# Gated feed-forward, last group: the order of the short pair and the full pairs

## The reference, cut to what matters

```python
x = layer_norm(ALPHA * x + merged @ w_out[l], ln1_g[l], ln1_b[l])
u = causal_dwconv(x @ w_up[l], f_conv_w[l], f_conv_b[l])
u_gate, u_val = jnp.split(u, 2, -1)
x = layer_norm(ALPHA * x + (jax.nn.silu(u_gate) * u_val) @ w_down[l], ln2_g[l], ln2_b[l])
```

## Time and profile before

| | |
|---|---|
| median of 3 runs | 2588.08 us |
| lowest, highest | 2584.64, 2588.22 us |
| span of the profiled execution | 2591.1 us |
| own time of the profiled execution | none given beside its span |
| PE, POOL, DVE, ACT busy | 97%, 60%, 53%, 26% of the span |
| mean granted clock of TensorE | 0.987 |

### The profile page before, as it was taken

How to read it: one execution, slowest core, us unless ns; L and a number is a source line. 1 busy time by engine, 2 the same in 40 slices (tenths; PEclk the granted TensorE clock), 3 DMA queues, 4 the chain that set the end, 5 groups by cost and what they waited for, 6 DMA issues and landing times.

```text
span 2591.1 us, 30721 instructions
## 1 busy us (share of the span) xinstructions
PE 2517.8 (97%) x11112; PEld 1992.6 (77%) x11112; DVE 1369.7 (53%) x1916; ACT 667.4 (26%) x1101; POOL 1563.9 (60%) x1061
## 2 busy tenths in 40 slices
PE   7999999999999999999999999999999999999998
PEld 6875688888877776688867886767888787888885
DVE  5975683221379999968214335444356134534344
ACT  3006621100254434421022114223114212200002
POOL 2640256766779898667633765624763567566663
PEclk8999999999999999999999999999999999999998
DMA  9620132233222322122320231312331223233221
GB/s 299 222 92 1 57 123 83 96 97 98 98 82 82 97 81 65 53 98 98 112 67 33 98 98 51 98 49 66 98 91 56 65 81 98 81 97 98 96 76 44
DMA packets 224141, 231.46 MB, mean 89 GB/s; under 512 B 12219, under 2 KB 213788, under 8 KB 223900
## 3 DMA queue, kind: packets, MB, share of 16 engines
q1 hardware_dynamic: 221104, 229.33, 28.0%
q10 hardware_dynamic: 2924, 0.66, 0.1%
HBM read 227.87 MB, written 2.10 MB: 89 GB/s over the span
## 4 chain that ended last, share of the span: by engine, by line
PE 85%; DVE 8%; DVEq 2%; ACT 2%; POOLq 1%; issue 1%; DMA 1%; POOL 0%; ACTq 0%; SPq 0%
PE PS L1540 64%; PE PS L1487 7%; PE PS L1348 3%; DVE PS L3076 3%; PE PS L2136 1%; DVEq L3078 1%; PE PS L1007 1%; PE PS L2338 1%; PE PS L2355 1%; PE PS L2127 1%; DVE PS L3120 1%; PE PS L2723 1%; DMA spare<-in_ada_w 1%; PE PS L1777 0%; POOLq L3065 0%
## 5 line engine op out<-in xcount | busy, mean ns | idle before, releaser
L1461 POOL TENSOR_TENSOR Wl<-raw,Wh 128x512 fp32r<-128x512 f32 (+2 forms) x764 | 1035.2, 1386 | 28.3 <-issue 4.1
L1455 POOL TENSOR_SCALAR Wh<-raw 128x2048 fp32r<-128x2048 f32 (+1 forms) x195 | 367.7, 1886 | 816.3 <-issue 378.4
L1540 PE MATMUL PS<-Hh,Wh 128*128 128x512 f32 x1936 | 765.5, 395 | 30.2 <-POOL Wl L1461 21.0
L1540 PE MATMUL PS<-Hl,Wh 128*128 128x512 f32 x1936 | 758.8, 392 | 0.0
L1540 PE MATMUL PS<-Hh,Wl 128*128 128x512 f32 x1936 | 758.1, 392 | 0.0
L1540 PEld LDWEIGHTS PS<-Hh,Wh 128*128 128x128 f32 x1936 | 366.2, 189 | 117.5 <-POOL Wl L1461 20.3
L1540 PEld LDWEIGHTS PS<-Hh,Wl 128*128 128x128 f32 x1936 | 366.2, 189 | 77.8
L1540 PEld LDWEIGHTS PS<-Hl,Wh 128*128 128x128 f32 x1936 | 366.5, 189 | 77.3 <-issue 1.7
L1540 PE MATMUL PS<-Bh,Wh 128*128 128x512 f32 x688 | 271.4, 394 | 2.7 <-DVE Bl L3372 2.1
L1540 PE MATMUL PS<-Bh,Wl 128*128 128x512 f32 x688 | 269.7, 392 | 0.0
L1540 PE MATMUL PS<-Bl,Wh 128*128 128x512 f32 x688 | 269.6, 392 | 0.0
(11 more groups left out here) (505 smaller groups left out, 3015.2 us busy)
## 6 DMA issues: line engine op xcount, KB each, us to landing
raw<-in_w_in SPq DMA_DIRECT2D x44, 1024.0 KB, 5.5
raw<-in_w_ff SPq DMA_DIRECT2D x32, 1024.0 KB, 5.3
raw<-in_conv_w_in SPq DMA_DIRECT2D x24, 1024.0 KB, 5.2
raw<-in_ret_w_in SPq DMA_DIRECT2D x24, 1024.0 KB, 5.1
spare<-in_ada_w SPq DMA_DIRECT2D x20, 1024.0 KB, 9.0
raw<-in_w_up SPq DMA_DIRECT2D x20, 1024.0 KB, 5.3
raw<-in_w_out SPq DMA_DIRECT2D x8, 1024.0 KB, 4.9
raw<-in_conv_w_out SPq DMA_DIRECT2D x8, 1024.0 KB, 5.0
```

Source lines behind the costliest of these rows:

```text
L1455: pool.tensor_scalar(st.Wh[0:rows, slot, k, 0:cols], st.raw_slot(slot)[0:rows, k, 0:cols], 1.0, 1.0, ALU.mult, ALU.mult)
L1461: ins = pool.tensor_tensor(st.Wl[0:rows, slot, k, 0:cols], st.raw_slot(slot)[0:rows, k, 0:cols], st.Wh[0:rows, slot, k, 0:cols].bitcast(F3 ...
L1540: mm = pe.matmul(out, lhs, rhs, start=(k == parts[0][0] and n == 0), stop=(k == parts[-1][0] and n == 2))
```

## The change

In a group with a rest the short pair is put ahead of the full pairs, and the down-projection of that group takes the chunks in the order 4, 0, 1, 2, 3, with the 64-row chunk 5 behind them as before. In groups without a rest nothing changes. The functions called (`pair`, `tiles`, `kparts`) are unchanged.

```diff
         ready = first_ready if g == 0 else None
-        segs = [pair(g, 0, full, TW, ready)]
-        if rem:
-            segs.append(pair(g, 2 * full, 1, rem, None, join=P < rem <= P + P // 2))
-
-        def made(k, segs=segs, full=full):
-            return segs[0].result_ready(k) if k < 2 * full else segs[1].result_ready(k - 2 * full)
-        steps += segs
-        steps.append(tiles(wd, B, 4, 0, row0=g * D, rows=rows, ready=made,
-                           dve=add_to_x(st, x_scale=ALPHA if g == 0 else 1.0)))
+        short = [pair(g, 2 * full, 1, rem, ready, join=P < rem <= P + P // 2)] if rem else []
+        long = pair(g, 0, full, TW, None if short else ready)
+
+        def made(k, long=long, short=short, full=full):
+            return long.result_ready(k) if k < 2 * full else short[0].result_ready(k - 2 * full)
+        steps += [*short, long]
+        down = tiles(wd, B, 4, 0, row0=g * D, rows=rows, ready=made,
+                     dve=add_to_x(st, x_scale=ALPHA if g == 0 else 1.0))
+        if short:
+            down.k_order = [2 * full, *range(2 * full)]
+        steps.append(down)
```

## The result

The changed kernel runs in 2591.81 us (median of 21 runs, 2588.72 to 2595.53), the kernel before, beside it, in 2588.38 (21 runs, 2584.58 to 2591.40). The ratio is 1.0014, 95% interval 1.0009 to 1.0020: slower by 3.4 us, a loss that 21 runs of each resolve and that is under the 0.2% named in the prediction. Forecast was 2591.8.

The account below looks back on a forecast made before the run. PE, busy 97% of the span, was taken as the bound. New costs of 10.0 us against 7.9 gave +2.1; 1.6 for runs lacking the old slow clock made +3.7: 2591.8 us, range 2587.3 to 2597.0.

Parts of the forecast that it names:

- (a): All queues: matmul, DVE, ACT and DMA work stays the same in number and shape; moved DMAs cost nothing.
- (b): First full gate tile: POOL's split has only the short value tile as cover; 2.04 us late, gap about 1.9.
- first rival: Clock turns a small loss into a visible one, by the old or new stalls; about +7 us, 2595, chance 0.34.
- (c): Before the last down-projection: the short pair's chain, 3.10 us, and POOL's stall there are removed.
- (d): First down tile: the last full pair's chain, 8.15 us, has 18 ready matmuls as cover; stall 4.07 us.
- (e): Last down tile: the normalisation's column sum moves from fourth to fifth place; cost 0.9 us, bounds 0 to 1.4.
- (f): Behind the new down-projection stall: PE runs at a slow clock; 3.0 us taken, between 1.6 and 4.8.
- the sum for the profiled execution: Whole change: costs of 10.0 us after against 7.9 before, so +2.1 us against the profiled execution.
- The 1.6: Clock behind the new stall: cost in us if dense work soon releases the throttle, by the skill's rule alone.
- two runs of three with a slow stretch: Kernel before, behind its old stall: the 4.8 us slow stretch counted in only these runs, which adds 1.6 us.
- The nearest rival: Clock turns the small loss into a visible one; about +7 us, 2595, chance 0.34.
- the one in which the full pairs' chain is the only cost: POOL's split ends in time and the column-sum delay is hidden; +0.8 us, 2588.9, chance 0.15.

Follow-up runs that it names:

- the repaired order: Changed kernel with early 64-row chunk, gate tile started by pairs of chunks, full pairs written out, column sum back in fourth place, seven fillers; 2582.69 us, ratio 0.9983.
- e4: Changed kernel with 15 small filler products on PE ahead of the wait for chunk 2 in the first down tile; 2588.18 us, ratio 1.0002.
- e5: Kernel before with 9 small filler products ahead of its wait for chunk 4 in the rest group's first down tile; 2585.12 us, ratio 0.9985.
- e6: Changed kernel with the two full pairs written out and the first full gate tile started on each pair of chunks once split; 2586.56 us, ratio 0.9994.
- e1: Changed kernel without its chunk order: short pair first, down-projection in the order 0, 1, 2, 3, 4, 5; 2593.34 us, ratio 1.0016 to the kernel before.
- e3: Changed kernel with the 64-row chunk 5 moved from last to second place, column sum still at fifth place; 2588.39 us, ratio 0.9999.
- e7: Kernel before with the copy of the 64 leftover rows behind the gate's filter instead of ahead of it; 2583.68 us, ratio 0.9986.
- e2: Changed kernel with the last norm's column sum issued ahead of chunk 2, fourth in the new order; 2590.15 us, ratio 1.0011.

## Why the prediction was right

(a) Moved loads and instructions cost next to nothing: no wait for a DMA shows near the change, and the repaired order is 0.5 us faster than its terms said. With the clock taken out of both (e4, e5) the change costs 4.2 us, and the terms below, as measured, add up to 2.13 + 4.07 + 0.86 - 3.10 = 4.0; the 0.2 between them has no cause that the runs show.

(b) POOL's split: 2.04 us of lateness and a gap of about 1.9 were forecast; the gap is 1.97, in five profiles, and the lateness 2.13 (the last matmul ahead of it starts at 2470.32, the next could start 0.23 later and starts at 2472.68). The 80-column tile of the earlier trace rows was the right row to read it from. None of these gaps of 1.97 was followed by a slow stretch; that part of the first rival did not occur in a profile. Since e6, without the gap, gained more in the median than in its stage, it isn't excluded for other executions.

(c) and (d): the stall shows as 3.92 and is 4.07 between slots, as worked out. The argument was a count of ready chunks against one measured chain, and e1 and e3 moved it both ways. Both chains had time to give: e7 took 0.7 us off the short pair's by moving one copy, and in e6, with the full pairs written out, theirs was 0.7 shorter.

(e) The column sum: 0.9 forecast, 0.86 measured, removed alone by e2.

(f) The clock: 3.0 taken, 2.5 measured in the profile after (e4). The size was near, but the reason given for it does not hold. The prediction took a value between a short and a long slow stretch because 64-row matmuls would come again behind the stall. The first of them started when the stretch was over:

```profile
2529.34 0.63 PE L1540 MATMUL PS<-Bh,Wl 128*128 128x512 f32 x1
2529.90 0.51 PE L1540 MATMUL PS<-Bh,Wh 64*128 64x512 f32 x1
```

All 12 matmuls ahead of it, the slow ones, have 128 rows. In e1 the clock is back by 2535.6 too, and its first 64-row matmul starts at 2537.04. The trace of before also held a row that was nearer than the earlier trace rows, and that the prediction passed over:

```profile
966.54 0.79 PE L1540 MATMUL PS<-Hh,Wh 128*128 128x512 f32 x1 [3.68 <-POOL Wl L1461]
...
971.00:972.00 1.00, 1.00 (x4) 0.50 0.01 2
972.00:973.00 1.00, 1.00 (x5) 0.63 0.00 0
```

Behind this gap, as long as that of the earlier trace rows, PE was slow for 6.2 us, on 128-row matmuls alone; at 0.48 of its length, an estimate from the earlier trace rows, that is 3.0 us. So two gaps of 3.7 us were followed by 3.1 and 6.2 slow microseconds, and 2.5 was one outcome of several: that it came out near 3.0 is in part luck. By the sum for the profiled execution the change was +2.1, and +1.9 was measured.

The Trainium skill, "TensorE: Matmul & The Clock Gate", section "What's actually happening", says that activity releases the throttle. The slow stretches behind this stall did end while PE was busy (at 2529.96 after, 2539.4 before). The 1.6 that the prediction drew from that rule alone was too low.

The step from the profile to the median was the least founded: two runs of three with a slow stretch. e5 gives 3.4 of 4.7 us between the medians, a share of 0.7 if the stretch is always that long, with the wide interval above. That makes the change 4.2 + 2.5 - 3.4 = 3.3 us slower, against 3.4 measured and 3.7 forecast; but the 2.5 is of one execution, and I don't know its spread. What a single execution shows can be off by as much as the whole effect: 4.7 us of the profile before hung on this one place. That forecast and result both read 2591.8 is luck: the difference came out 0.3 smaller than forecast, and the median of the kernel before 0.3 higher than in the three runs of the prediction.

One thing that I told wrongly ahead of the result: the last down-projection is written out, not looped. No term used it. The nearest rival, the clock turning the loss into a visible one at +7, lies outside the interval of the ratio, as does the one in which the full pairs' chain is the only cost (+0.8).

What stays open: why the clock falls behind or inside one gap and not another, and why PE was then slow for 3.1, 5.4, 6.2 or 10 us. Where in the stall the clock fell explains a part: 1.3 us of the low clock were idle time in the profile after. That 64-row matmuls prolong a slow stretch is ruled out for those of 5.4 and 6.2 us, which had none; for the one of 10 us no run isolates it.

## What to carry to other kernels

When a result is consumed in chunks, count the ready chunks in slots of the consumer and set them against the whole chain from producer to post; an order that hides one wait shows at once which it opens. Follow every hook that is keyed to a chunk's number when the order of chunks changes. A narrow tile is a poor cover: the work of another engine for the tile behind it doesn't shrink with it. And where TensorE stalls for about 2 us, look at the granted clock behind the stall before looking at the stall: shortening the chain by 0.7 us was worth 5.5 in the stage, one profile against another, and 3.6 (1.3 to 6.0) by the ratio.

## What the hardware showed

A stall of 2.14 us cost 4.7 us in the clock, besides its own length, and one of 3.92 us only 2.5: the price doesn't follow the length of the stall. In the second the clock had fallen 1.3 us before the stall ended, and that part was free. Gaps of 1.4, 1.97 and 2.11 us left the clock at 1.00 in the profiles taken here, the one of 2.14 did not; so close together, they give no bound below which a gap is safe. Fillers of constants into an unused bank (15 of them, 30 instructions in 3.5 us) kept it at 1.00 through a stall of 3.9 (e4).
